# Twenty gate and up panels of the last FFN as seven quarter products instead of eight

## What is computed

```python
def swiglu(x, w_in, w_out):
    a, b = jnp.split(x @ w_in, 2, axis=-1)
    return (jax.nn.silu(a) * b) @ w_out

h = h + 0.5 * g3 * swiglu(modulate(h, norm_ffn2[layer], sh3, sc3), w_ffn2_in[layer], w_ffn2_out[layer])
return rmsnorm(h, final_norm)
```

## Time and profile before

| | |
|---|---|
| median of three runs | 3048.46 us (3047.97 to 3048.81) |
| span of the profiled execution | 3046.0 us |
| TensorE matmul busy | 3018.3 us, 14862 matmuls |
| VectorE busy | 1497.2 us |
| ScalarE busy | 1020.8 us |
| GpSimd busy | 287.1 us |
| last FFN's matmuls | 2672.6 to 3033.7 us |

### The profile page before, as it was taken

The page is one execution under the profiler, slowest core; times in us unless marked ns, Lnnn a source line. Parts: engine busy times, 40 slices in busy tenths (PEclk is TensorE's granted clock), DMA queues, the critical chain, the costliest instruction groups (busy, mean ns, idle before and its releaser), DMA issues.

```text
span 3046.0 us, 35091 instructions
## 1 busy us (share of the span) xinstructions
PE 3018.3 (99%) x14862; PEld 2440.4 (80%) x14862; DVE 1497.2 (49%) x2267; ACT 1020.8 (34%) x1529; POOL 287.1 (9%) x223
## 2 busy tenths in 40 slices
PE   9999999999999999999999999999999999999998
PEld 6767888877667888878888888888888888878887
DVE  4565333354655334362222325576878794443333
ACT  4553222234533233241111124443333335232222
POOL 0233000011232000010000001010101021000000
PEclk9999999999999999999999999999999999999999
DMA  5113442322124322221211112121212133322222
GB/s 186 44 56 152 180 148 96 104 95 77 42 99 186 146 97 90 90 84 56 70 56 65 68 54 99 56 88 58 92 54 97 49 108 127 126 78 104 100 91 75
DMA packets 45051, 285.08 MB, mean 94 GB/s; under 512 B 5135, under 2 KB 5663, under 8 KB 19424
## 3 DMA queue, kind: packets, MB, share of 16 engines
q1 hardware_dynamic: 42480, 269.77, 24.8%
q0 software_dynamic: 2416, 13.09, 1.2%
HBM read 277.04 MB, written 5.79 MB: 93 GB/s over the span
## 4 chain that ended last, share of the span: by engine, by line
PE 94%; DVE 3%; ACT 1%; POOL 1%; issue 0%; DMA 0%; DVEq 0%; SPq 0%; POOLq 0%; ACTq 0%
PE ps L765 28%; PE ps L766 28%; PE ps L767 28%; PE ps L854 2%; PE ps L933 2%; PE ps L946 1%; PE ps L960 1%; PE ps L839 1%; DVE CA L2003 1%; POOL tmp_a L2240 1%; PE ps L845 0%; DVE wlo L1637 0%; PE ps L940 0%; DVE A1l L1660 0%; PE ps L787 0%
## 5 line engine op out<-in xcount | busy, mean ns | idle before, releaser
L765 PE MATMUL ps<-A1h,whi 128*128 128x512 f32 x2240 | 886.2, 396 | 9.0 <-DVE A1l L1656 7.4
L767 PE MATMUL ps<-A1h,wlo 128*128 128x512 f32 x2240 | 873.3, 390 | 0.0
L766 PE MATMUL ps<-A1l,whi 128*128 128x512 f32 x2240 | 873.3, 390 | 0.0
L1637 DVE TENSOR_TENSOR wlo<-wraw,whi 128x2048 fp32r<-128x2048 f32 (+2 forms) x221 | 465.0, 2104 | 270.1 <-ACT whi L1174 270.1
L1174 ACT ACTIVATE whi<-wraw 128x2048 fp32r<-128x2048 f32 (+2 forms) x221 | 385.0, 1742 | 480.9 <-PE ps L767 463.1
L765 PEld LDWEIGHTS ps<-A1h,whi 128*128 128x128 f32 x2240 | 421.9, 188 | 103.2 <-issue 14.1
L767 PEld LDWEIGHTS ps<-A1h,wlo 128*128 128x128 f32 x2240 | 421.0, 188 | 88.9
L766 PEld LDWEIGHTS ps<-A1l,whi 128*128 128x128 f32 x2240 | 421.5, 188 | 85.4 <-issue 2.2
L1813 DVE TENSOR_TENSOR SIL<-SIL,ps 128x512 f32<-128x512 f32 (+1 forms) x110 | 69.7, 634 | 575.6 <-PE ps L767 492.5
L1350 ACT ACTIVATE SIL<-ps 128x512 f32<-128x512 f32 (+1 forms) x110 | 61.0, 555 | 701.2 <-PE ps L767 698.6
L2003 DVE SCALAR_TENSOR_TENSOR CA<-YIN,vec,CA 128x512 f32<-128x512 f32 x238 | 191.7, 805 | 6.9
(11 more groups left out here) (389 smaller groups left out, 4407.8 us busy)
## 6 DMA issues: line engine op xcount, KB each, us to landing
wraw<-wstream SPq DMA_DIRECT2D x159, 1024.0 KB, 4.8
MW<-wstream SPq DMA_DIRECT2D x34, 1024.0 KB, 6.5
wraw<-wstream SPq DMA_DIRECT2D x42, 768.0 KB, 4.2
wraw<-wstream SPq DMA_DIRECT2D x34, 640.0 KB, 3.9
wraw<-wstream SPq DMA_DIRECT2D x4, 960.0 KB, 4.6
hk<-gd POOLq DMA_DIRECT2D x1, 2560.0 KB, 13.3
X<-xT SPq DMA_DIRECT2D x4, 512.0 KB, 7.0
sx<-X POOLq DMA_DIRECT2D x1, 2048.0 KB, 7.6
```

The source lines that it names most:

```text
L765: mm(o, l[0], r[0], start=start, stop=False)
L766: mm(o, l[0], r[1], start=False, stop=False)
L767: return mm(o, l[1], r[0], start=False, stop=stop)
L1637: tt(wlo[i_ % 2][:, 0:n], wraw[i_ % 2][:, 0:n], raw(whi[i_ % 2][:, 0:n]), SUB).then_inc(ev("lo", i_).by(dve_wlo), 1)
```

## The change

**The products.** Let a panel's weights be cut in four quarters: gate or up, by the first or last four blocks of the width; the tokens' tiles likewise in four: first or last four blocks, first or last 256 tokens. The eight products of quarters become seven, by a scheme of Strassen's kind, for panels 2 to 21 of `f3` (`SEVEN = {"f3": 2}`). Each product is a `block` of 12 matmuls of 256 columns. Panels 0 and 1 and the down panels stay as they were.

**The operands.** Four mixed token quarters are formed once: ScalarE writes each token tile a second time, unrounded, into `B3` (`whole`); VectorE takes four differences in place, ScalarE rounds them (`T3h`), VectorE forms the low part (`T3l`). Four mixed weight quarters are formed for each panel by GpSimd (`mix`: four adds of 128x512 from `wraw` into `M3`), rounded by ScalarE (`mixed_high`, 2048 columns), and VectorE forms their low part (`mixed_low`, 2048 columns). `M3` is one buffer, and starts where `B3` lies; the rounded pairs `E3` are two. The load into a `wraw` buffer waits for the last of the four sums too. Weight panels are laid out by quarters.

**The sums.** The first product of a panel goes into bank 4, the fifth into bank 5. ScalarE seeds the panel's two banks with the first (`seed`), copies the sixth's sum to the gate bank (`seed_gate`), the seventh's to the other half of the up bank (`seed_up`), and keeps the fifth (`keep_fifth`, two buffers); VectorE adds the fifth to two halves at the end (`add_fifth`). Silu and the multiplication of a panel come one panel later than before.

**The order.** The first product of panel j + 1 stands ahead of the last product of panel j; for the first panel of a group (`leader`) it stands between the two tiles of the last down panel, which are computed one after the other (`apart`) for that. GpSimd's `mix` calls stand ahead of its last adds of squares. The two late modulation buffers move, and modulation products of `f3` take banks 4 to 7.

```diff
@@ def tensor(e):
-            def apart(p, op, tiles, names, k0=0, group=0):
+            def apart(p, op, tiles, names, k0=0, group=0, between=None):
                 for t, name in zip(tiles, names):
+                    if between and t == tiles[-1]:
+                        between()
...
+            def seven(name, op):
+                def block(o, weights, moving, start=False):
+                    for k in range(4):
+                        w, x = weights(k), moving(k)
+                        mm(o, w[0], x[0], start=start and k == 0, stop=False, skip_group_check=True)
+                        mm(o, w[0], x[1], start=False, stop=False, skip_group_check=True)
+                        last = mm(o, w[1], x[0], start=False, stop=k == 3, skip_group_check=True)
+                    return last
...
+                def first(j):
+                    i, one = index["gu", name, j], pin(4, "one", name, j)
+                    e.wait_ge(one.before, ev("lo", i))
+                    block(one.ap[:, 0:256], own(i, 1), tokens(0, 0), True).then_inc(one.full.by(product), 1)
+                def fifth(j):
+                    five = pin(5, "five", name, j)
+                    e.wait_ge(five.before, ev("mix lo", name, j), ev("tokens lo", name, 0))
+                    block(five.ap[:, 0:256], mixed(j, 1), mixed_tokens(0, 0), True).then_inc(five.full.by(product), 1)
+                def others(j, opening):
+                    i, (g, u) = index["gu", name, j], gate_banks(name, j)
+                    if opening:
+                        fifth(j)
+                    e.wait_ge(ev("seeded", name, j))
+                    block(g.ap[:, 0:256], own(i, 0), tokens(4, 0))
+                    e.wait_ge(ev("mix lo", name, j), ev("tokens lo", name, 1))
+                    block(u.ap[:, 256:512], mixed(j, 2), mixed_tokens(4, 256)).then_inc(ev("sixth", name, j).by(product), 1)
+                    if not opening:
+                        fifth(j)
+                    e.wait_ge(ev("gate seeded", name, j))
+                    block(u.ap[:, 256:512], mixed(j, 0), mixed_tokens(0, 256)).then_inc(ev("seventh", name, j).by(product), 1)
+                    block(g.ap[:, 256:512], mixed(j, 3), tokens(4, 256)).then_inc(ev("used mix", name, j).by(product), 1)
+                    if (name, j) in follower:
+                        first(follower[name, j])
+                    e.wait_ge(ev("up seeded", name, j))
+                    block(u.ap[:, 0:256], own(i, 2), mixed_tokens(4, 0)).then_inc(u.full.by(product), 1)
+                    used(Panel(("gu", name, j)), u.full)
...
@@ def scalar(e), emit:
+                    if whole is not None:
+                        act(whole[:, c, :], tmp[:, c % 3, 0:n], ACT.Identity, bias=bias(c), scale=1.0).then_inc(
+                            ev("whole", op.name, c).by(act_out), 1)
...
+            def seven(name, op, hid, ring, last):
+                def mixed_high(j):
+                    e.wait_ge(ev("mixed", name, j, 3), ev("used mix", name, j - 2) if j > SEVEN[name] + 1 else PB.of("modp", 35).full)
+                    act(E3[j % 2][0][:, :, :], M3[:, :, :], ACT.Copy, bias=0.0, scale=1.0).then_inc(ev("mix hi", name, j).by(act_whi), 1)
...
+                for k in range(0, 8, 4):
+                    e.wait_ge(ev("tokens", name, 3 if k else 1), PB.of("modp", 35).full)
+                    act(T3[0][:, k:k + 4, :], B3[:, k:k + 4, :], ACT.Copy, bias=0.0, scale=1.0).then_inc(ev("tokens hi", name, k // 4).by(act_out), 1)
+                for g, js in enumerate(HIDDEN):
+                    for jj, j in enumerate(js):
+                        at("gu", name, j)
+                        after = j + 1 if j + 1 == leader[name, g] else follower.get((name, j))
...
+                        behind = j > leader[name, g]
+                        if behind:
+                            silu(j - 1)
+                        if j == SEVEN[name]:
+                            keep_fifth(j)
+                        seed_gate(j)
+                        if after:
+                            mixed_high(after)
+                        if j > SEVEN[name]:
+                            keep_fifth(j)
+                        seed_up(j)
+                        if behind:
+                            gated(j - 1, jj - 1, g)
+                        if after:
+                            seed(after)
...
@@ def vector(e):
+                tt(b11, b11, b12, SUB).then_inc(ev("tokens", name, 0).by(dve_out), 1)
+                tt(b12, b22, b12, SUB).then_inc(ev("tokens", name, 1).by(dve_out), 1)
...
+                for k in range(0, 8, 4):
+                    e.wait_ge(ev("tokens hi", name, k // 4))
+                    tt(T3[1][:, k:k + 4, :], B3[:, k:k + 4, :], raw(T3[0][:, k:k + 4, :]), SUB).then_inc(ev("tokens lo", name, k // 4).by(dve_out), 1)
...
+                        if behind:
+                            add_fifth(j - 1)
+                        at("gu", name, j)
...
+                        if behind:
+                            gate(j - 1)
+                        if after:
+                            mixed_low(after)
+                        if behind:
+                            hidden(j - 1, jj - 1, g)
...
@@ def gpsimd(e):
+            def mix(j):
+                i = index["gu", "f3", j]
+                w = wraw[i % 2]
+                quarter = [w[:, 512 * q:512 * q + 512] for q in range(4)]
+                e.wait_ge(ev("w landed", i), ev("mix lo", "f3", j - 1) if j > SEVEN["f3"] else ev("tokens lo", "f3", 1))
+                tt(M3[:, 1, :], quarter[3], quarter[2], ADD).then_inc(ev("mixed", "f3", j, 0).by(pool_out), 1)
+                tt(M3[:, 0, :], quarter[1], quarter[3], ADD).then_inc(ev("mixed", "f3", j, 1).by(pool_out), 1)
+                e.wait_ge(ev("mixed", "f3", j, 0))
+                tt(M3[:, 2, :], M3[:, 1, :], quarter[1], ADD).then_inc(ev("mixed", "f3", j, 2).by(pool_out), 1)
+                e.wait_ge(ev("mixed", "f3", j, 2))
+                tt(M3[:, 3, :], M3[:, 2, :], quarter[0], ADD).then_inc(ev("mixed", "f3", j, 3).by(pool_out), 1)
...
@@ def sync(e), load:
-                    e.wait_ge(ev("lo", i - 2))
+                    e.wait_ge(ev("lo", i - 2), ev("mixed", *stream[i - 2]["key"][1:], 3) if stream[i - 2]["quarters"] else None)
```

More of the change, by code:

```diff
@@ L21 @@
 HIDDEN = [range(0, 6), range(6, 12), range(12, 17), range(17, 22)]
+SEVEN = {"f3": 2}
 CONV_W = 31
@@ L513, in build, with pin @@
         uses, clock = {}, [0]
-        banks = [Cell(ctx.enter_context(nc.psum_tensor(f"ps{i}", [128, 512], F32))[:, :]) for i in range(8)]
+        ps = ctx.enter_context(nc.psum_tensor("ps", [128, 4096], F32))
+        banks = [Cell(ps[:, 512 * i:512 * i + 512]) for i in range(8)]
         PB, OB, AB, ZB = (Ring(x, uses, clock) for x in (banks[:4], banks[4:], banks[:7], banks[7:]))
+        def pin(i, *key):
+            if key not in uses:
+                c = banks[i]
+                clock[0] += 1
+                c.at = clock[0]
+                c.use = uses[key] = Use(c.ap, c.use.free)
+            return uses[key]
         wraw = [sb(f"wraw{i}", [128, 2048], 8 * i) for i in range(2)]
@@ L713, in build, with gate_banks, halves, down_banks @@
         assert not left
+        slot, follower, leader = {}, {}, {}
+        for name, first in SEVEN.items():
+            n = 0
+            for g, js in enumerate(HIDDEN):
+                own = [j for j in js if j >= first]
+                leader[name, g] = own[0]
+                for j in js:
+                    slot[name, j] = n
+                    n += 1
+                for j, after in zip(own, own[1:]):
+                    follower[name, j] = after
+                for f in range(0, 8, 2):
+                    slot[name, g, f] = n
+                    n += 1
+        def gate_banks(name, j):
+            i = 2 * (slot[name, j] % 2)
+            return pin(i, "gate", name, "x", j), pin(i + 1, "up", name, "x", j)
+        def halves(name, j):
+            i = 1024 * (slot[name, j] % 2)
+            return ps[:, i:i + 1024].rearrange("p (a b) -> p a b", b=256)
+        def down_banks(name, g, f):
+            for i in range(2):
+                pin(2 * (slot[name, g, f] % 2) + i, "dn", name, "x", g, f + i)
         def mod_ready(i):
@@ L1026, in ffn @@
             def ffn(name, streams, between=None, beside=None):
+                if name in SEVEN:
+                    first, others = seven(name, streams[0][1])
                 for g, js in enumerate(HIDDEN):
@@ L1037, in ffn @@
                         hid = dict((t, hid) for t, _, hid in streams)[tag]
-                        each = apart if (g, f, tag) == (3, 6, "x") else two
-                        each(panel("down", name, g, f), hid, (0, 1), [("dn", name, tag, g, f), ("dn", name, tag, g, f + 1)], group=g)
+                        opens = name in SEVEN and f == 6 and g < 3
+                        each = apart if opens or (g, f, tag) == (3, 6, "x") else two
+                        if name in SEVEN:
```

(7 more changed lines are left out.)

149 lines of the change are left out of this document (134 added, 15 removed).

## The result

| | before | after |
|---|---|---|
| median | 3047.97 us (3047.30 to 3048.81) | 3058.82 us (3058.10 to 3059.78) |
| ratio | | 1.0035, 95% interval 1.0023 to 1.0048 |
| span of the profiled execution | 3046.0 | 3057.0 |
| TensorE matmul busy | 3018.3 | 3007.6 |

What follows compares the result with a forecast made beforehand. TensorE was taken as the bound, busy 3018.3 of 3046.0 us. Entry +12.5, boundaries +2.2, other groups -6.4 gave +8.3: span 3054.3, median 3056.8, said as 3057; 8-in-10 range 3041 to 3072.

Steps and rivals of the forecast that it cites:

- The price of a product: Twenty new panels: 256-column matmuls step 0.120 us, so 10.08 us a panel instead of 10.90; 0.80 saved each, 16 at most.
- The second rival: New blocks: 256-wide step of 0.109 us and turns don't matter, total 3036 us; chance 0.06.
- The entry: Start of the last FFN through group 0: token and weight preparation delays TensorE; 12.5 us lost.
- TensorE panel 1 from 2687.0: Entry: panel 1's matmuls run from 2687.0 to 2697.9, against a start of 2685.39 in the old kernel.
- the chain that I had summed: Entry, VectorE's queue with GpSimd's sums: TensorE waits 5.1 us for panel 2's low part, 4.0 for its mixed low.
- The loop with turns: Mixing, panel to panel: VectorE and GpSimd alternate by whole instructions, loop exceeds 10.08 us; three later groups still gain 6.4.
- With both the loop is 11.9: Mixing loop: 9.5 us plus turns of 0.55 and 2.1 taken by VectorE, so TensorE must wait.
- late seeds: Panels 3, 4, 9, 10, 15 and 20: last product waits 1.5 to 2 us for ScalarE's seed.
- m: End of a panel's four sums from its start; TensorE free under 5.9; later groups foretold 2.9, 5.6, 7.5, 7.75.
- the first rival: Mixing loop: turns don't matter, loop 9.5 to 10.05 us, no panel waits in it; total 3044 us, chance 0.20.
- The boundaries: Last down panel before each following group: first product waits for leader's low part, 0.5, 0.5 and 1.2; 2.2 us lost.
- The slow clock: Entry: the 5.1 us wait can lower the granted clock, blocks taking twice as long; bound 0 to +3 us.

Runs made afterwards that it cites:

- The best kernel: Changed kernel with modulation banks moved, seven products from panel 3, early mixed panel, two sum buffers, 1536-column parts, panel 2's parts before mixed-token rounding: 3036.36 us, 0.9963.
- The second edit of experiments 8 to 11: Kernel with modulation banks moved and seven products from panel 3, plus first mixed panel's high part before silu, low part before gate: 3045.80 us, 0.9990.
- experiment 1: Changed kernel with modulation products just ahead of the last FFN taking banks 4 to 7: 3050.72 us, 1.0008 of before.
- experiment 3: Changed kernel with high and low parts of seven-product panels formed for 1536 columns, not 2048: 3054.86 us, 1.0022 of before.

## Why the prediction was right, and where it was not

Forecast 3057, slower by 0.3%; measured 3058.8, slower by 0.35%. Two of its terms were wrong, by 7.0 us one way and by 4.4 the other. That the total is off by only 1.8 us is luck; the shape of the loss (little won per panel, the entry as the largest term) was right.

**The price of a product: right.** The new blocks step by 0.120 us, like the context stream; three of them in after:

```profile
2800.10 0.28 PE L1067 MATMUL ps<-A1l,E3h 128*128 128x256 f32 x1
2800.22 0.28 PE L1068 MATMUL ps<-A1h,E3l 128*128 128x256 f32 x1
2800.34 0.28 PE L1066 MATMUL ps<-A1h,E3h 128*128 128x256 f32 x1
```

The best kernel gains 11.8 us where nineteen panels at 0.80 give 15.2. The second rival (a step of 0.109) falls.

**The entry: wrong.** The step that failed is "TensorE panel 1 from 2687.0". The sum had TensorE in panel 0 as each token tile came; its only look at banks was that those of the down panels are free in time, and a wait for the pinned banks of panel 0 was put at nothing without a reason. TensorE stood still until 2686.28, ran slowly behind that, and began panel 1 here:

```profile
2699.86 0.49 PE L814 MATMUL ps<-A1h,whi 128*128 128x512 f32 x1
```

That is 12.9 us later than foretold. Behind it the chain that I had summed was mostly hidden: no wait for panel 2's low part, where I had 5.1, and 2.7 for the mixed low part, where I had 4.0. The 2.7 have another cause than my 4.0. The sums had ended at 2700.48, but ScalarE's `mixed_high` stands behind the silu of panel 1 (L1463) and could begin only with it done, at 2710.90:

```profile
2710.40 0.60 ACT L1463 ACTIVATE SIL<-ps 128x512 f32<-128x512 f32 x1 [7.14 <-PE ps L816]
2710.90 1.91 ACT L1472 ACTIVATE E3h<-M 128x2048 fp32r<-128x2048 f32 x1
```

The second edit of experiments 8 to 11 changes that order, and it took away a wait of 2.8. What I wrote for the chain holds in kind in experiment 1, with the bank free: waits of 4.7, 2.5, 0.5 and seeds late by 0.4 and 1.6, group 0 ending 11.3 us later than before (foretold 5.1, 4.0, 0.7, 0.6 to 1.8, and 12.5). The 11.3 hold 1.5 us of slow clock behind the wait of 2.5, which the 12.5 did not, so the chain itself was priced some 3 us too dear. The mechanism was there, as the second in line; the first one I hadn't seen, and it cost 7 us more. The miss for the mixed low (2.5 for 4.0) is that the sums began at 2695.41, not 2696.55.

**The loop with turns: right in kind, too strong.** (The sum in "With both the loop is 11.9" gives 12.15; nothing else uses it.) Foretold were late seeds in six panels; there are three, of 0.78, 1.64 and 1.40 us, in the second and third new panel of group 0 and the fifth of group 1. Groups 2 and 3 have none. The time grows from panel to panel as said, but one step later. GpSimd's adds in group 1 (timeline, after):

```profile
2804.09 1.30 POOL L2535 TENSOR_TENSOR M<-M,wraw 128x512 f32<-128x512 f32 x1
2805.47 1.29 POOL L2537 TENSOR_TENSOR M<-M,wraw 128x512 f32<-128x512 f32 x1
...
2816.06 1.30 POOL L2537 TENSOR_TENSOR M<-M,wraw 128x512 f32<-128x512 f32 x1
...
2826.65 3.22 POOL L2537 TENSOR_TENSOR M<-M,wraw 128x512 f32<-128x512 f32 x1
...
2837.11 3.35 POOL L2535 TENSOR_TENSOR M<-M,wraw 128x512 f32<-128x512 f32 x1
```

In the third panel of the group I had VectorE's subtraction before the last add. The add began at 2816.06, the subtraction at 2816.23, and it was VectorE that waited (3.27 us). GpSimd lost no turn there, so m went 2.8, 3.3, 5.8, 7.7, not 2.9, 5.6, 7.5, 7.75. By this reading 0.17 us of order decided whether a group of five loses 1.5 us; no run moves that order by itself. In groups 2 and 3 m reached 5.77, just under the 5.9 at which the forecast and the first rival part, so they ended as the first rival has it. It made the three later groups 4.4 us better than foretold.

**The boundaries: right.** Waits with their restart of 0.47, 0.48 and 1.15, foretold 0.5, 0.5 and 1.2, and gone when the leader's low part is shorter by a quarter.

**The rest.** The four 1024-wide instructions took 1.22 each (interpolated 1.2), the copies within PSUM 0.37 (taken 0.36, bound 0.63). The slow clock, which the sum held at nothing and the bounds at "0 to +3", cost 3.8 us in after (2.3 and 1.5). That the loop and not TensorE sets the time held only for the first product of panel 2 in experiment 1: it ran 1.2 us longer, and the wait behind it was shorter by that. Its blocks took 1.8 times as long (0.213 by 0.120), not twice. Of the matmul of 0.63 us in the earlier trace rows the trace of before doesn't show that it ran at the lower level; the 0.63 at a granted clock of 0.50 in after does show that length. Loads were hidden everywhere.

## What to carry to other kernels

A saving of 7% on a saturated engine needs every helper's instructions placed in time: sum each engine's queue in its order, at the entry of the stage first, since there the helpers have no panel of lead. When a ring that gives out the longest-free bank is replaced by fixed banks, list for each fixed bank its last reader and what stands ahead of that reader in its queue. And a helper loop that fits its period by half a microsecond with one buffer (9.5 of 10.08 here) should get its second buffer before it is timed.

## What was new about the hardware

VectorE and GpSimd hold each other up by whole instructions when both read from SBUF, in either direction: a subtraction of 2.29 us takes up to 3.44, an add of 1.29 up to 3.42. Writing alone on GpSimd doesn't do it, even for 5.43 us of every 10. And the granted clock was at the lower level behind waits of 14.6, 4.6, 2.8 and 2.7 us; behind that of 4.6 the first 4.5 us of matmuls ran at a mean granted clock of 0.62, which is 1.7 us (4.5 x 0.38) on top of the wait. Behind another wait of 2.7 us, in experiment 3, it was not (1.00 from 2714.70 to 2718.00).
